# The feed-forward's pair scheme: the weight sums move from GpSimd to VectorE, and the pairs begin at block 6 instead of 8

## The reference

```python
def sqrelu_mlp(h, w1, w2):
    return jnp.square(jax.nn.relu(h @ w1)) @ w2
# x = x + sqrelu_mlp(rms_norm_2(x, norm_ffn[i]), ffn_w1[i], ffn_w2[i])
```

## Time and profile before

| | us |
|---|---|
| median of the runs (2618.2, 2622.53, 2624.03) | 2622.53 |
| the profiled execution | 2618.97 |
| its span, first to last instruction | 2617.2 |
| PE busy in it | 2580.0 |
| DVE busy | 1687.4 |
| ACT busy | 1286.9 |
| POOL busy | 505.9 |

### The profile page before, as it was taken

The page is one execution under the profiler, slowest core; times in us unless marked ns, Lnnn a source line. Parts: engine busy times, 40 slices in busy tenths (PEclk is TensorE's granted clock), DMA queues, the critical chain, the costliest instruction groups (busy, mean ns, idle before and its releaser), DMA issues. The chain is left out here.

```text
span 2617.2 us, 35132 instructions
## 1 busy us (share of the span) xinstructions
PE 2580.0 (99%) x12530; PEld 2044.8 (78%) x12530; DVE 1687.4 (64%) x2288; ACT 1286.9 (49%) x2138; POOL 505.9 (19%) x366
## 2 busy tenths in 40 slices
PE   9999999999999999999999999999999999999999
PEld 7855788888786557788888776789988787889887
DVE  4476677643988785677653787588743536688633
ACT  3326543333547894444333587457533424557432
POOL 0020100000104781100000130035810002045800
PEclk9999999999999999999999999999999999999999
DMA  5320222222234442222222220133232321223222
GB/s 212 105 80 17 100 96 97 97 98 96 81 131 129 121 129 80 82 96 96 96 97 96 95 73 1 58 105 113 81 110 97 102 88 52 94 108 114 81 96 96
DMA packets 72991, 248.39 MB, mean 95 GB/s; under 512 B 8076, under 2 KB 8204, under 8 KB 72496
## 3 DMA queue, kind: packets, MB, share of 16 engines
q1 hardware_dynamic: 71792, 238.53, 27.2%
q0 software_dynamic: 944, 8.40, 0.9%
q10 hardware_dynamic: 144, 0.00, 0.0%
HBM read 242.56 MB, written 2.24 MB: 94 GB/s over the span
## 5 line engine op out<-in xcount | busy, mean ns | idle before, releaser
L356 DVE TENSOR_TENSOR wlo<-wraw,whi 128x1024 fp32r<-128x1024 f32 x353 | 454.9, 1290 | 421.1 <-ACT whi L333 420.0
L382 PE MATMUL bank<-hnhi,whi 128*128 128x512 f32 (+1 forms) x1664 | 654.0, 393 | 2.0 <-DVE arena L1972 1.2
L383 PE MATMUL bank<-hnlo,whi 128*128 128x512 f32 (+1 forms) x1664 | 638.3, 384 | 0.0
L333 ACT ACTIVATE whi<-wraw 128x1024 fp32r<-128x1024 f32 x361 | 380.1, 1055 | 485.3 <-DMA wraw<-in_w 485.1
L384 PE MATMUL bank<-hnhi,wlo 128*128 128x512 f32 x1536 | 598.5, 390 | 0.0
L382 PE MATMUL bank<-ahi,whi 128*128 128x512 f32 x1184 | 463.1, 391 | 0.9 <-DVE alo L605 0.4
L384 PE MATMUL bank<-ahi,wlo 128*128 128x512 f32 x1184 | 460.8, 389 | 0.0
L383 PE MATMUL bank<-alo,whi 128*128 128x512 f32 x1184 | 460.7, 389 | 0.0
L382 PEld LDWEIGHTS bank<-hnhi,whi 128*128 128x128 f32 x1664 | 312.7, 188 | 93.7 <-issue 32.8
L383 PEld LDWEIGHTS bank<-hnlo,whi 128*128 128x128 f32 x1664 | 312.9, 188 | 63.8 <-issue 4.8
L384 PEld LDWEIGHTS bank<-hnhi,wlo 128*128 128x128 f32 x1536 | 288.3, 188 | 61.8
(11 more groups left out here) (351 smaller groups left out, 3908.8 us busy)
## 6 DMA issues: line engine op xcount, KB each, us to landing
wraw<-in_w SPq DMA_DIRECT2D x410, 512.0 KB, 3.3
arena<-cs_scratch SPq DMA_DIRECT2D x20, 512.0 KB, 5.7
over_a<-cs_scratch SPq DMA_DIRECT2D x12, 512.0 KB, 5.9
arena<-in_rpb POOLq DMA_DIRECT2D x1, 2880.0 KB, 14.1
out_dram<-xT SPq DMA_DIRECT2D x8, 256.0 KB, 2.0
arena<-in_t_step POOLq DMA_DIRECT2D x2, 897.0 KB, 5.7
mT<-arena SPq DMA_DIRECT2D x28, 64.0 KB, 2.0
arena<-in_t_ab POOLq DMA_DIRECT2D x1, 1472.0 KB, 6.7
```

What stands on the lines that cost most here:

```text
L333: act.activation(whi[:, slot * BLOCK:(slot + 1) * BLOCK], wraw[:, slot * BLOCK:(slot + 1) * BLOCK], ACT.Copy).then_inc(sem("w_hi"), 1)
L356: dve.tensor_tensor(low_home(i), wraw[:, slot * BLOCK:(slot + 1) * BLOCK], whi[:, slot * BLOCK:(slot + 1) * BLOCK], ALU.subtract).then_inc ...
L382: pe.matmul(out, wh, ah, start=start, stop=False)
L383: pe.matmul(out, wh, al, start=False, stop=False)
```

## The change

Three things are changed together.

1. `PLAIN` is 6 and not 8: six plain blocks and 13 pairs for each feed-forward. The places that the first pairs' quarters take over change with it, and so does the order in which the down-projection takes its first banks.
2. The weight sums of all pairs are made by DVE (`block_sum`), placed one by one between its low parts. One count, `SUMS`, numbers all of DVE's sums. Blocks of later pairs are loaded when DVE's low parts are done, without a wait for POOL.
3. POOL keeps t1 and the scalings. With the sums gone, nothing stands ahead of the scalings in its list but t1 and the norm's scale.

DVE's list before the pairs changes: the low parts of blocks 6 and 7 (1024 wide) go, and after relu 4 come eight instructions for pair 0; the low part of t4 moves into the first pair. ACT's list changes alike.

```diff
-PLAIN = 8
+PLAIN = 6
@@ pool_pairs
-            for n in range(PAIRS):
-                wait_block(pool, f, n, 0)
-                wait_block(pool, f, n, 1)
...
-                pool.tensor_tensor(sum_raw("s4"), block_raw(f, n, "a12"), sum_raw("s2"), ALU.subtract)\
-                    .then_inc(sem("sum_pool"), 1)
             pool.wait_ge(sem("norm_rstd"), 6 + 2 * f)
@@ sp_pairs
-                sp.wait_ge(sem("w_lo"), split(f, "a22", n))
-                sp.wait_ge(sem("sum_pool"), pool_summed(f, "s4", n))
+                sp.wait_ge(sem("w_lo"), max(split(f, q, n) for q in ("a11", "a12", "a22")))
@@ act_mlp_up
-                elif m <= 5:
+                elif m <= 3:
                     act_next(act, name, At(m))
...
+                if m == 4:
+                    high("a11", 0)
+                    high("s1", 0)
+                    high("a22", 0)
+                if m == 5:
+                    high("a12", 0)
                 hidden_square(m)
-                if m == 4:
+                if m == 3:
                     token_high("t2")
                     token_high("t4")
@@ dve_mlp_up
+            def block_sum(q, n):
+                if n >= PAIRS:
+                    return
+                if q == "s1":
+                    wait_block(dve, f, n, 0)
+                    wait_block(dve, f, n, 1)
+                else:
+                    dve.wait_ge(sem("sum_dve"), summed(f, {"s2": "s1", "s3": "s2", "s4": "s2"}[q], n))
+                if n:
+                    dve.wait_ge(sem("w_lo"), split(f, q, n - 1))
+                a, b, op = {"s1": (block_raw(f, n, "a21"), block_raw(f, n, "a22"), ALU.add),
+                            "s2": (sum_raw("s1"), block_raw(f, n, "a11"), ALU.subtract),
+                            "s3": (block_raw(f, n, "a11"), block_raw(f, n, "a21"), ALU.subtract),
+                            "s4": (block_raw(f, n, "a12"), sum_raw("s2"), ALU.subtract)}[q]
+                dve.tensor_tensor(sum_raw(q), a, b, op).then_inc(sem("sum_dve"), 1)
...
-                elif m <= 5:
+                elif m <= 3:
                     dve_next(dve, name, At(m))
                 wait_up(dve, name, At(m))
                 dve.tensor_scalar(tile(m), bank[m % 4][:, :], 0.0, None, ALU.max).then_inc(sem("mlp_relu"), 1)
...
-                if m == 5:
+                if m == 4:
+                    block_sum("s1", 0)
+                    low("a11", 0)
+                    block_sum("s2", 0)
+                    low("s1", 0)
+                    block_sum("s3", 0)
+                    block_sum("s4", 0)
+                    low("a22", 0)
                     token_lows("t2")
-                    token_lows("t4")
-                if m == 6:
-                    low("a11", 0)
-                    low("s1", 0)
             low("a12", 0)
             for n in range(PAIRS):
                 if n > 1:
                     sum_w(n - 1)
+                if n:
+                    block_sum("s1", n + 1)
                 low("s2", n)
                 if n == 0:
-                    low("a22", 0)
+                    block_sum("s1", 1)
                 if n + 1 < PAIRS:
                     low("a11", n + 1)
+                    block_sum("s2", n + 1)
                     low("s1", n + 1)
                 if n:
                     sum_c(n - 1)
                 low("s3", n)
                 if n == 0:
                     sum_w(0)
+                block_sum("s3", n + 1)
                 low("s4", n)
                 if n + 1 < PAIRS:
                     low("a12", n + 1)
                 else:
                     dve_split(dve, At(FIRST[f"mlp_down{f}"]))
+                block_sum("s4", n + 1)
+                if n == 0:
+                    token_lows("t4")
                 if n + 1 < PAIRS:
                     low("a22", n + 1)
```

More of the change, by code:

```diff
@@ L873, in build @@
                                                                            (("a22", c - 1), ("s2", c))))])
-        SPLIT = pair_counts([s for c in range(PAIRS) for s in (before(("a11", 0), ("s1", 0), ("a12", 0)) if c == 0 else [])
-                             + [("s2", c)] + (before(("a22", 0)) if c == 0 else [])
-                             + before(("a11", c + 1), ("s1", c + 1), ("s3", c), ("s4", c), ("a12", c + 1), ("a22", c + 1))])
+        SPLIT = pair_counts([(q, 0) for q in ("a11", "s1", "a22", "a12")]
+                            + [s for c in range(PAIRS) for s in [("s2", c)] + before(
+                                ("a11", c + 1), ("s1", c + 1), ("s3", c), ("s4", c), ("a12", c + 1), ("a22", c + 1))])
         def first_pair(f):
@@ L891, in relu_done, with summed @@
             return 32 * f + m + 1
-        POOL_SUMS, COPIES, DVE_SUMS = 1 + 4 * PAIRS + MLP_TILES, 5 + 2 * PAIRS, 7 + 2 * PAIRS
+        POOL_SUMS, COPIES = 1 + MLP_TILES, 5 + 2 * PAIRS
         TOKEN_SUMS = ("t3", "t1", "t2", "t4")
         SUM_AT = {"s1": 0, "s2": 1, "s3": 2, "s4": 3}
-        def pool_summed(f, q, n):
-            return POOL_SUMS * f + 1 + 4 * n + SUM_AT[q] + 1
+        SUMS = pair_counts([
+            ("t3", None), ("t2", None), ("t4", None), ("low t3", None), ("low t1", None), ("s1", 0), ("s2", 0), ("s3", 0),
+            ("s4", 0), ("low t2", None), ("s1", 1), ("s2", 1), ("w", 0), ("s3", 1), ("s4", 1), ("low t4", None)]
+            + [s for c in range(1, PAIRS + 1) for s in ([("w", c - 1)] if c > 1 else []) + before(
+                ("s1", c + 1), ("s2", c + 1)) + [("c", c - 1)] + before(("s3", c + 1), ("s4", c + 1))])
+        def summed(f, what, n=None):
+            return len(SUMS) * f + SUMS[what, n]
         def hidden_scaled(f, m):
-            return POOL_SUMS * f + 1 + 4 * PAIRS + m + 1
+            return POOL_SUMS * f + 1 + m + 1
         def z_copied(f, n):
@@ L938, in quarter_hi @@
         def quarter_hi(f, q, n):
-            freed, half = {"a11": (4, 0), "s1": (4, 1), "a12": (5, 0), "s2": (5, 1), "s3": (6, 0), "s4": (6, 1),
-                           "a22": (7, n % 2)}[q]
+            freed, half = {"a11": (4, 0), "s1": (4, 1), "a12": (5, 0), "s2": (5, 1), "s3": (2, 0), "s4": (2, 1),
+                           "a22": (3, n % 2)}[q]
             a = (FIRST[f"mlp_up{f}"] + freed) % 4 * BLOCK + half * QUARTER
@@ L1023, in high @@
                 if n == 0 or (q, n) == ("a22", 1):
-                    act.wait_ge(sem("w_used"), plain_used(f, {"a11": 4, "s1": 4, "a12": 5, "s2": 5, "s3": 6, "s4": 6, "a22": 7}[q]))
+                    act.wait_ge(sem("w_used"), plain_used(f, {"a11": 4, "s1": 4, "a12": 5, "s2": 5, "s3": 2, "s4": 2, "a22": 3}[q]))
                 else:
@@ L1230, in product @@
                 if t and n == 0:
-                    pe.wait_ge(sem("sum_dve"), token_low(f, t))
+                    pe.wait_ge(sem("sum_dve"), summed(f, "low " + t))
                 for j in range(4):
```

65 lines of the change are left out of this document (15 added, 50 removed).

## The result

The changed kernel takes **2625.85 us** (median of 20 runs), the kernel before 2620.6 (20 runs): ratio 1.002, 95% interval 1.0013 to 1.0026. That is 5.25 us slower; the forecast was 5.1. (The three runs of the kernel before on which the forecast of 2627.6 stands had a median of 2622.5; it carries their 1.9 us.) The profiled execution has a span of 2622.8 us. The page's first part shows what moved between the engines: POOL lost 158 us, and PE has 72 more matmuls, since in each feed-forward 48 of 512 columns have become 84 of 256. DVE hardly changed, though it has 104 new sums: with POOL's sums gone, it is held up by them no more. In the 20 us of steady pairs its 18 instructions took 16.83 us before; at the pace of 0.60 and 0.33 us they would take 9.7 (an estimate: 14 x 0.60 + 4 x 0.33).

What follows compares the result with a forecast made beforehand. PE, busy 2580.0 of 2617.2 us, was taken to bound the kernel. Its own work, late starts and the old losses removed, -1.6 + 2 x (5.95 + 0.4) - 5.96 = +5.1, on 2622.5 gave 2627.6 us; range 2616 to 2636.

Steps and rivals of the forecast that it cites:

- PE's own work, -1.6 us: Moving from block 8 to 6 makes two plain blocks a pair in each feed-forward: 2 x 0.80 = 1.6 us less.
- A weight sum on DVE, 0.60 us: Not in the earlier trace; taken as a low part of the same shape, 0.60 us, between 0.55 and 0.69.
- What POOL costs DVE, 5.05 us before relu 5: Before the pairs, POOL's early scalings hold up DVE, 1.0 to 1.2 us per operation, 5.05 us in all.
- Relu 5 at 1739.0, a stand of 4.1 us: At the start of the pairs DVE finishes relu 5 at 1739.0; PE, wanting it from 1734.85, stands 4.1 us.
- From relu 5 to `sum_c(0)`, 13.35 us: DVE's list in the first pair: 12.0 us of instructions plus 1.35 of waiting, so `sum_c(0)` is done at 1752.35.
- a22(0) 5.95 us late: In the first pair PE starts a22(0) 5.95 us late, waiting for `sum_c(0)`, the stand for relu 5 included.
- `sum_w(1)`, 0.4: PE's wait for the second pair's `sum_w`, put at 0 or 0.8 us and taken as 0.4.
- Steady pairs hold: In steady pairs DVE has 9.6 of 10.08 us, so it barely keeps up and PE has no gap.
- The sum, +5.1: Whole kernel: -1.6 + 2 x (5.95 + 0.4) - 5.96 = +5.1 us, slower than before.
- Where DVE is in time: Rival: scalings fall into DVE's waits, relu 5 ready near 1734 to 1735; -4.0 us, 2618.5; chance 0.20.
- Scalings that don't disturb: Rival: POOL's scalings don't hold up DVE though the scheme starts earlier; -5.2 us, 2617; chance 0.05.
- bound steady pairs: Rival: DVE bounds the steady pairs at 10.75 us each, 0.67 over PE; +15 us, 2642; chance 0.10.

Runs made afterwards that it cites:

- e9: The kernel of e8 with the pairs beginning at block 8 instead of block 6: 2614.0 us, ratio 0.9976.
- e8: The changed kernel with two DVE sums, `sum_c(0)` and `sum_w(1)`, moved ahead and POOL's scalings after all pairs: 2612.38 us, ratio 0.9969.
- e1_lag: The changed kernel with POOL's scalings six tiles later, DVE's list as it is: 2616.82 us, ratio 0.9986.
- e10: The kernel of e8 with POOL's first five scalings put back early, beside the plain blocks: 2621.26 us, ratio 1.0006.
- e4_order_lag: The changed kernel with DVE's and ACT's lists reordered around the first pair and the scalings six tiles later: 2625.66 us, ratio 1.0018.

## Why the prediction was right, point by point

- **PE's own work, -1.6 us.** Right: 1.62 us by the stages of e9 against e8. The steady pair still takes 10.08 us (POOL's first scaling of a pair at 1784.58 and 1794.66).
- **A weight sum on DVE, 0.60 us.** Right: from 1733.07 to the next at 1733.67, and over all of one line of it:

```profile
L1140 DVE TENSOR_TENSOR over_a<-over_a,wraw x26: 674/678/684, 1733.1 to 2423.1; 128x512 f32<-128x512 f32 x26
```

(the columns are the shortest, median and longest in ns: 0.68 us with the 0.08 that overlaps the next).

- **What POOL costs DVE, 5.05 us before relu 5.** Right in kind, too large. Measured: 0.32 at the low part of block 4 (1.55 against 1.23), 2.08 at the tokens, 0.5 at s1(0) (1.18 against 0.68), 1.10 at s4(0): 4.0 us. The term most mis-sized is scaling 3: it waited beside the low parts of t3 and t1 (2.68 us for itself) and took only 0.5 from DVE, and not 1.15. The two at the tokens took 0.3 less than the 2.4 allowed.
- **Relu 5 at 1739.0, a stand of 4.1 us.** 1739.0 in a trace that is 1.0 us later, thus 1738.0; the gaps are 3.21 and 3.08 us.
- **From relu 5 to `sum_c(0)`, 13.35 us.** Measured 14.0 in stage 1 (from 1739.0 to 1752.98, the end of `sum_c(0)` by its pace) and 13.3 in stage 2. The difference is a stand that the prediction didn't have. PE is in its slow stretch, so DVE waits 0.57 us for it ahead of `sum_w(0)`; in stage 2, at full clock, it doesn't.
- **a22(0) 5.95 us late.** By the paces it would start 31.80 us after the row from which the stage is counted (18.84 to the end of block 5, then nine products of 1.44). It starts 5.75 us later than that in stage 1 and 4.97 in stage 2. The slow stretch of stage 1 is hidden in the second gap, as foreseen (0.97 us there and 1.78 in stage 2), but for these 0.57 us.
- **`sum_w(1)`, 0.4.** 0.62 us in both, as large as in the earlier trace rows.
- **Steady pairs hold.** Right: no gap. DVE has 8.8 us a pair and not 9.6, since the first of the two scalings (1784.58) falls mostly into the 1.03 us that DVE waits for ACT's high part of a12.
- **The sum, +5.1.** With the measured terms in it, it is -1.6 + (5.75 + 0.61) + (4.97 + 0.62) - 5.96 = +4.4, and the stages show 4.3. The two late starts were 1.2 us too large together, the two `sum_w(1)` 0.4 too small. The medians differ by 5.25, 0.9 more than the stages of the two profiles, and no run shows where that lies. So the mechanism was right, and that the forecast meets the medians to 0.15 us is in part luck. The 5.96 us of before's losses are also those of one profile, with a slow stretch that not every execution need have.

- **The rivals.** Where DVE is in time, -4.0 was forecast; e1_lag makes that case and comes to -3.7, with gaps of 1.1 us at a22(0) and 0.7 at s3(1) where the rival had 1.8 and none. Scalings that don't disturb are excluded by e10, bound steady pairs and a scheme without gain by the unbroken 10.08 us and by e9.

The chances had faster, same and slower at 0.13, 0.43 and 0.44: the measured 0.2%, with an interval clear of no change, lies on the edge between the last two.

## What to carry to other kernels

When work leaves an in-order engine's list, ask what stood behind it there: no line of the scalings was edited, but they moved from a place where DVE had nothing late to the place where it was latest. An engine that owes work at a hand-over should neither stand nor be held up by another engine until the debt is paid; moving the wanted item to the front helps only if the engine doesn't wait for it. With two more edits that follow this (the scalings behind the pairs, two of DVE's sums ahead), the change gives 8 us (0.31%) instead of costing 5.

## What the runs showed of the hardware

DVE instructions with two SBUF operands and POOL's scalings and sums don't run at the same time here; one waits for the other. Mostly they take turns: scaling 4 (1734.39) took 1.71 us and the DVE sum behind it 1.78, where alone they take 1.29 and 0.68. Scaling 3 (1729.32) did not get its turn between two long DVE operations. It took 2.68 us while both kept their pace, and 2.68 again in the second up-projection. A relu from PSUM kept 0.68 us beside scaling 3.

The table has ten PE gaps of 3.08 to 3.44 us. Nine of them were followed by a stretch partly at 1.2 GHz (granted clock 0.66 over five us, over ten in e4_order_lag); the exception is the changed kernel's 3.08 us in stage 2, with 1.00 behind it. Of the five gaps of 1.78 to 1.98 us one was followed by such a stretch, in the kernel before, and of the shorter ones none. A stretch cost 1.5 to 1.6 us in the matmuls, and 2.7 in e4_order_lag.
